# Hybrid encoder trunk, the scan: one predicated copy joins a level's inverse and its transpose; the opening merge is issued earlier

## The reference, cut to what matters

```python
L = jnp.where(strict, jnp.einsum('bhnik,bhnjk->bhnij', k_beta, k) * decay, 0.0)
sol = lax.linalg.triangular_solve(eye + L, rhs, left_side=True, lower=True)
...
def step(S, inp):                      # RWKV-7
    r_t, w_t, k_t, v_t, a_t, b_t = inp
    Sa = jnp.einsum('bhvk,bhk->bhv', S, a_t)
    S = S * w_t[:, :, None, :] + Sa[..., None] * b_t[:, :, None, :] + v_t[..., None] * k_t[:, :, None, :]
    return S, jnp.einsum('bhvk,bhk->bhv', S, r_t)
```

## Time and profile before

| | |
|---|---|
| runs | 4060.42, 4061.81, 4055.37 us; median 4060.42 |
| profiled execution | 4057.4 us, its span 4055.6 us |
| TensorE busy | 3793.7 us, 94% of the span |
| VectorE busy | 2142.2 us, 53% |
| ScalarE busy | 1305.0 us, 32% |
| GpSimd busy | 900.6 us, 22% |
| mean granted clock of TensorE | 0.965 of full speed |
| joins of the scan | 688.3 to 1410.3 us from the span's start |

### The profile page before, as it was taken

One profiled execution on the slowest core, in us unless ns is written; L12 is line 12 of the kernel. 1 busy time (PEld: TensorE's weight loads), 2 busy tenths in 40 slices (PEclk: granted clock), 3 DMA queues, 4 the chain that ended last, 5 costly groups with the idle time before them and its releaser, 6 DMA issues. The chain is left out here.

```text
span 4055.6 us, 74164 instructions
## 1 busy us (share of the span) xinstructions
PE 3793.7 (94%) x31136; PEld 3237.2 (80%) x31136; DVE 2142.2 (53%) x3226; ACT 1305.0 (32%) x2304; POOL 900.6 (22%) x472
## 2 busy tenths in 40 slices
PE   7999975999999988999999997899989899999998
PEld 6888854888888867888888886788868788888887
DVE  5644286767767785434333346566643343433335
ACT  3321274444344443111111114355533211111112
POOL 1231174111111033111111112134422211111113
PEclk8999976999999989999999997999999999999999
DMA  4322495222222152101101113000022110110112
GB/s 120 92 83 82 141 345 195 75 70 70 75 70 70 44 193 82 42 31 41 41 32 41 41 42 113 9 8 13 1 89 83 47 42 31 41 41 32 41 41 104
DMA packets 193526, 289.37 MB, mean 71 GB/s; under 512 B 31216, under 2 KB 134448, under 8 KB 193296
## 3 DMA queue, kind: packets, MB, share of 16 engines
q1 hardware_dynamic: 193296, 286.02, 21.1%
HBM read 207.99 MB, written 77.99 MB: 71 GB/s over the span
## 5 line engine op out<-in xcount | busy, mean ns | idle before, releaser
L847 DVE TENSOR_TENSOR top_acc<-top_acc,ffn_down 128x512 f32<-128x512 f32 x600 | 412.4, 687 | 358.4 <-PE ffn_down L112 357.7
L110 PE MATMUL ffn_up<-hT_ffn_high,ffn_w_high 128*128 128x512 f32 (+1 forms) x1536 | 544.0, 354 | 4.9 <-DVE hT_ffn_low L809 4.9
L112 PE MATMUL ffn_up<-hT_ffn_high,ffn_w_low 128*128 128x512 f32 (+1 forms) x1536 | 543.8, 354 | 0.0
L111 PE MATMUL ffn_up<-hT_ffn_low,ffn_w_high 128*128 128x512 f32 (+1 forms) x1536 | 543.5, 354 | 0.0
L110 PE MATMUL ffn_down<-ffn_w_high,ffn_f_high 128*128 128x512 f32 x1280 | 498.6, 390 | 0.0
L111 PE MATMUL ffn_down<-ffn_w_low,ffn_f_high 128*128 128x512 f32 x1280 | 498.3, 389 | 0.0
L112 PE MATMUL ffn_down<-ffn_w_high,ffn_f_low 128*128 128x512 f32 x1280 | 497.9, 389 | 0.0
L836 DVE TENSOR_TENSOR ffn_square<-ffn_relu 128x512 f32<-128x512 f32 (+1 forms) x192 | 146.6, 764 | 640.8 <-ACT ffn_relu L762 640.8
L110 PEld LDWEIGHTS ffn_up<-hT_ffn_high,ffn_w_high 128*128 128x128 f32 x1536 | 290.6, 189 | 46.3 <-issue 5.3
L111 PEld LDWEIGHTS ffn_up<-hT_ffn_low,ffn_w_high 128*128 128x128 f32 x1536 | 290.6, 189 | 40.9
L112 PEld LDWEIGHTS ffn_up<-hT_ffn_high,ffn_w_low 128*128 128x128 f32 x1536 | 290.5, 189 | 40.0
(11 more groups left out here) (477 smaller groups left out, 7948.7 us busy)
## 6 DMA issues: line engine op xcount, KB each, us to landing
up_w_raw<-in_w_ff SPq DMA_DIRECT2D x64, 1024.0 KB, 5.1
s_tm_both<-prepare_tb SPq DMA_DIRECT2D x20, 512.0 KB, 6.7
s_fm_dir<-prepare_fd SPq DMA_DIRECT2D x20, 512.0 KB, 6.9
scan_tb<-s_tm_both SPq DMA_DIRECT2D x20, 512.0 KB, 3.7
scan_fb<-s_fm_both SPq DMA_DIRECT2D x20, 512.0 KB, 4.8
scan_fd<-s_fm_dir SPq DMA_DIRECT2D x20, 512.0 KB, 5.9
up_w_raw<-s_x SPq DMA_DIRECT2D x20, 512.0 KB, 4.8
top_acc<-in_w_in_even SPq DMA_DIRECT2D x18, 512.0 KB, 5.5
```

The costliest lines, as they stand in the source:

```text
L110: pe.matmul(out, stationary[0], moving[0], start=start, stop=False)
L111: pe.matmul(out, stationary[0], moving[1], start=False, stop=False)
L112: return pe.matmul(out, stationary[1], moving[0], start=False, stop=stop)
L847: dve.tensor_tensor(a, a, out_of(u), ALU.add).then_inc(added, 1)
```

## The change

The two halves of X and of XT become one tensor of a quad, `XX`, in the order X half 0, XT half 0, X half 1, XT half 1. In this order the mixed pieces of X and of XT, and also the fixed ones, can be walked by one address pattern. Both products of a level go into one bank, the XT product behind the X product, and one `copy_predicated` of 128x512 joins both. Units alternate between banks 2 and 3, and so do the levels of quad 0. Four semaphores become two (`joined`, `g_joined`), and one wait for the bank two units back takes the place of two. The mask is kept once and repeated by the address pattern. In the opening `g_first` stands ahead of GpSimd's wait for `cleared`; of the seven tiles that VectorE cleared, ScalarE takes four, after its `decay_exp`.

```diff
-    Xp = [E.sb(f"X{q}", [P, 2, GR, HALF]) for q in range(Q)]
-    XTp = [E.sb(f"XT{q}", [P, 2, GR, HALF]) for q in range(Q)]
+    XX = [E.sb(f"X{q}", [P, 2, 2, GR, HALF]) for q in range(Q)]
+    Xp, XTp = [x[:, :, 0, :, :] for x in XX], [x[:, :, 1, :, :] for x in XX]
+    STRIDE = 2 * BLOCK
...
-    CLEARED = 27
-    DVE_TILES = 7
+    CLEARED = 28
+    DVE_TILES, ACT_TILES = 3, 7
...
+    def joint_halves(q, m):
+
+        n, rows = 1 << m, XX[q][:, :, :, :, :]
+        return bass.AP(rows.tensor, rows.offset + STRIDE, [rows.ap[0], [HALF, 2 * GR], [2 * n, HALF // (2 * n)], [n - STRIDE, 2], [1, n]])
+
+    def joint_mask(m):
+
+        n, rows = 1 << m, both_levels[:, m, :].bitcast(I32)
+        return bass.AP(rows.tensor, rows.offset, [rows.ap[0], [0, 2 * GR], [2 * n, HALF // (2 * n)], [n, 2], [1, n]])
+
+    def g_bank(m):
+
+        return 3 - m % 2
...
+    def joint_blocks(bank, m):
+
+        return ps[:, bank, 0:2 * BLOCK].rearrange("p (h a b n) -> p h a b n", h=2 * GR, b=2, n=1 << m)
...
                 if m < LAST:
-                    level(2, inner_blocks[0], gYc).then_inc(s["gz_product"], 1)
-                    level(3, gYc, inner_blocks[0]).then_inc(s["gzt_product"], 1)
+                    level(g_bank(m), 0, inner_blocks[0], gYc)
+                    level(g_bank(m), BLOCK, gYc, inner_blocks[0]).then_inc(s["gzt_product"], 1)
...
-                    pe.wait_ge(s["x_joined"], X_UNITS * i + u - RQ + 1)
+                    pe.wait_ge(s["joined"], UNITS * i + u - RQ + 1)
...
+                if u >= RQ:
+                    pe.wait_ge(s["joined"], UNITS * i + u - RQ + 1)
                 if m < LAST:
-                    if u > 0:
-                        pe.wait_ge(s["x_joined"], X_UNITS * i + u)
-                    level(2, inner_blocks[1 + u % 2], Y[u % 2]).then_inc(s["z_product"], 1)
-                if u > 0:
-                    pe.wait_ge(s["xt_joined"], UNITS * i + u)
-                if m < LAST:
-                    level(3, Y[u % 2], inner_blocks[1 + u % 2]).then_inc(s["zt_product"], 1)
+                    level(2 + u % 2, 0, inner_blocks[1 + u % 2], Y[u % 2])
+                    level(2 + u % 2, BLOCK, Y[u % 2], inner_blocks[1 + u % 2]).then_inc(s["zt_product"], 1)
...
-            act.activation(out[:, DVE_TILES:TILES, :].rearrange("p t (a n) -> p (t a) n", n=P), bcm(ident[:, :], (TILES - DVE_TILES) * D // P),
-                           ACT.Copy, scale=0.0).then_inc(s["cleared"], 1)
+            def clear_out(tiles):
+                act.activation(out[:, tiles, :].rearrange("p t (a n) -> p (t a) n", n=P), bcm(ident[:, :], (tiles.stop - tiles.start) * D // P),
+                               ACT.Copy, scale=0.0).then_inc(s["cleared"], 1)
+
+            clear_out(slice(ACT_TILES, TILES))
...
             for d in range(2):
                 decay_exp(0, 0, d)
+            clear_out(slice(DVE_TILES, ACT_TILES))
...
+            g_first(0, 0)
             pool.wait_ge(s["cleared"], CLEARED)
-            g_first(0, 0)
...
-            def join(x, bank, m):
-                return dve.copy_predicated(x, in_halves(both_levels[:, m, :, :], m).bitcast(I32), in_halves(out_blocks(bank), m))
+            def join(q, bank, m):
+                return dve.copy_predicated(joint_halves(q, m), joint_mask(m), joint_blocks(bank, m))
...
                 m, q = unit(u)
-                if m < LAST:
-                    dve.wait_ge(s["z_product"], X_UNITS * i + u + 1)
-                    join(x_halves(q, m), 2, m).then_inc(s["x_joined"], 1)
                 dve.wait_ge(s["zt_product"], UNITS * i + u + 1)
...
-                join(xt_halves(q, m), 3, m).then_inc(s["xt_joined"], 1)
+                join(q, 2 + u % 2, m).then_inc(s["joined"], 1)
```

More of the change, by code:

```diff
@@ L1470, in in_halves, with mixed_halves, out_block @@
         return ap.rearrange("p h (a b n) -> p (h a) b n", b=2, n=1 << m)
[L1472 removed]
+    def mixed_halves(pair, m, h=None, part=slice(0, P)):
         n, rows = 1 << m, pair[part, :, :, :]
         at, blocks = (0, BLOCK // (2 * n)) if h is None else (h * HALF, HALF // (2 * n))
[L1476 to L1477 removed]
+        return bass.AP(rows.tensor, rows.offset + STRIDE + at, [rows.ap[0], [2 * n, blocks], [n - STRIDE, 2], [1, n]])
     def x_halves(q, m, h=None, part=slice(0, P)):
[L1481 removed]
+        return mixed_halves(Xp[q], m, h, part)
     def xt_halves(q, m, h=None, part=slice(0, P)):
[L1485 removed]
+        return mixed_halves(XTp[q], m, h, part)
+    def joint_halves(q, m):
[6 more added lines that the diff above has]
+        return 3 - m % 2
     def both_columns(ap):
         return ap.rearrange("p h (a n) -> p (h a) n", n=HALF)
[L1491 to L1493 removed]
+    def out_block(bank, h, part, at=0):
+        return ps[part, bank, at + h * HALF:at + (h + 1) * HALF]
+    def joint_blocks(bank, m):
+        return ps[:, bank, 0:2 * BLOCK].rearrange("p (h a b n) -> p h a b n", h=2 * GR, b=2, n=1 << m)
     def out_blocks(bank, part=slice(0, P)):
@@ L1503, in last_xt @@
     def last_xt(q, h):
-        return XTp[q][UPPER, slot[0], h, :], XTp[q][LOWER, slot[1], h, :]
+        return XTp[q][UPPER, 1 - slot[0], h, :], XTp[q][LOWER, 1 - slot[1], h, :]
     def fixed_columns(pair, first, part=slice(0, P)):
         rows = pair[part, :, :, :]
-        step = BLOCK if first == 0 else -BLOCK
-        return bass.AP(rows.tensor, rows.offset + first * BLOCK, [rows.ap[0], [HALF, GR], [2, HALF // 2], [step + 1, 2]])
+        step = STRIDE if first == 0 else -STRIDE
+        return bass.AP(rows.tensor, rows.offset + first * STRIDE, [rows.ap[0], [HALF, GR], [2, HALF // 2], [step + 1, 2]])
     def ident_columns():
@@ L1597, in level_y, with level @@
                 return last
-            def level(bank, stationary, moving):
+            def level(bank, at, stationary, moving):
                 for h in range(GR):
                     for part in (LOWER, UPPER):
-                        last = pe.matmul(out_block(bank, h, part), stationary[part, h, :], moving[part, h, :], start=True, stop=True)
+                        last = pe.matmul(out_block(bank, h, part, at), stationary[part, h, :], moving[part, h, :], start=True, stop=True)
                 return last
@@ L1610, in last_y, with last_zt @@
                 return last
-            def last_zt(q, y):
+            def last_zt(q, y, bank):
                 for h in range(GR):
                     xt_fwd, xt_bwd = last_xt(q, h)
-                    pe.matmul(out_block(3, h, LOWER), y[UPPER, h, :], xt_fwd, start=True, stop=True)
-                    last = pe.matmul(out_block(3, h, UPPER), y[LOWER, h, :], xt_bwd, start=True, stop=True)
+                    pe.matmul(out_block(bank, h, LOWER), y[UPPER, h, :], xt_fwd, start=True, stop=True)
+                    last = pe.matmul(out_block(bank, h, UPPER), y[LOWER, h, :], xt_bwd, start=True, stop=True)
                 return last
@@ L3622, in constants @@
     row, column = s % mid, np.arange(mid)[None, :]
-    c["c_both_levels"] = np.stack([np.tile(row >> m == (column >> m) ^ 1, (1, 4)) for m in range(LEVELS - 1)]) * 1.0
+    c["c_both_levels"] = np.stack([row >> m == (column >> m) ^ 1 for m in range(LEVELS - 1)]) * 1.0
     keep = np.ones((2, P, TILES))
```

64 lines of the change are left out of this document (30 added, 34 removed).

## The result

The changed kernel takes **4077.17 us** (median of 5 runs, 4076.54 to 4081.13), against 4060.42 before: a ratio of 1.0044 with a 95% interval of 1.0033 to 1.0055. It is slower by 16.8 us, where 12.4 were forecast. The profiled execution took 4077.05 us with a span of 4075.3, 19.7 more than the span before.

The account below looks back on a forecast made before the run. It took the scan to be bound by TensorE's queue with short holes. 7.6 + 9.2 + 1 + 3.6 - 8.0 - 1 = +12.4 us gave 4072.8 against the median, slower at 0.57; the range takes in 4056 to 4084.

Parts of the forecast that it names:

- Price of the joint copy: VectorE's 128x512 join: result after 0.72 us, next start after 0.62; at the first level 1.2 and 1.05.
- Steps (1) to (3): Tail of a turn, g group's levels 3 to 5: later joins delay VectorE's masked copies 0.84 us, 7.6 over nine crossings.
- Steps (4) and (5): Units 0 and 1: Y of units 2 and 3 start 1.65 and 1.76 us later; ten times 0.92, 9.2 us.
- Step (6): Later units: nothing added or recovered; the last product's 0.59 us hole goes, worth 0 because the queue waits for GpSimd's merge.
- The last turn, +1: End of the scan: nothing fills the gaps of units 7 to 9 and one chain wait of 0.75 shows; +1 us.
- The opening's moved merge: Opening: GpSimd's merge starts 7.5 us sooner and its three instructions save 0.9 more; -8.0 us taken.
- The opening's chain, +3.6: Opening's levels: joint copies delay Y of level 2 by 1.3 us, later levels by 1.0, 0.75 and 0.54; +3.6 us.
- the clock, -1: Opening: TensorE's shorter idle stretch can bring the full clock sooner, taking back 1 of some 3 us.
- The rival of an opening that pays for the joins: No change, chance 0.28: two-element pieces cost nothing in the joint copy, so +2.7 us in all, 4063.1.
- That of a faster VectorE: Chance 0.15: VectorE sets the pace for part of a turn and joint copies pace below 0.62 us; 4038 us.

Follow-up runs that it names:

- two_copies: The changed kernel with its layout and opening, but X and XT of every level again in two banks with a copy each; 4051.52 us.
- group_split: The changed kernel with two copies in two banks for the g group's levels alone, the units keeping the joint copy; 4064.97 us.
- late_y: The kernel with two copies a level and the changed layout and opening, but Y's wait moved to the second (XT) copy; 4063.81 us.
- joint_only: The changed kernel with the opening of the kernel before; 4088.44 us.
- busy_opening: The changed kernel with 16 unread matmuls added in the opening, 11 ahead of the first product and 5 ahead of Y; 4072.79 us.
- opening_only: The kernel before with the change's opening alone, two copies a level in two banks staying; 4052.22 us.
- narrow_split: The changed kernel with two copies in two banks for the units' first level alone; 4070.66 us.
- fill_ahead: The changed kernel with 11 unread matmuls added ahead of the opening's first product alone; 4077.53 us.
- fill_between: The changed kernel with 5 unread matmuls added before Y of the opening's levels alone; 4073.29 us.
- busy_best: The kernel before with the change's opening alone, plus 16 unread matmuls in that opening; 4050.24 us, and 4050.66 when run again.

## Why the prediction came out as it did

The direction, the range and the mechanism of a turn were right; 12.4 us were forecast and 16.8 measured. By its own steps:

- **Price of the joint copy** (0.72 result and 0.62 pace; 1.2 and 1.05 at the first level): 0.73 and 0.63, 1.28 and 1.06 to 1.09. Right. The Trainium skill's "Vector Engine (DVE) Microarchitecture Reference" (5.2) would have runs of two adjacent words, if they start on an 8-byte boundary, at the full rate; the joint copy's rows speak against it. The Trainium skill's "VectorE: DVE Perf Modes" (TRN2 errata) has a fixed cost for each instruction with a source in SBUF (here the mask), not for every instruction as the prediction put it. In the pace of these rows one instruction fewer saves 0.05 us (two of 0.34 against 0.63), and with all 150 back two_copies is faster, since VectorE is not the bound.
- **Steps (1) to (3), +0.84 in the tail:** VectorE's masked copies start 29.39 behind KD instead of 28.42, +0.97, and group_split takes just that away. The join of level 4 started 0.46 late and not 0.28, so Y of level 4 was 0.77 late instead of 0.58. Shown besides, by late_y, is that the wide copy does this and not TensorE's wait.
- **Steps (4) and (5), +1.65 and +1.76:** Y of unit 2 is at 42.75 behind KD against about 40.92, +1.83, and Y of unit 3 at 46.51 against 44.54, +1.97. Of this 1.00 arises at the units (0.92 forecast). Nothing is recovered behind it, as said in (6).
- **Step (6), the last product's hole worth 0:** shown by two_copies, where the hole is gone and the turn is the same.
- **The last turn, +1 beside the turn's own loss:** too small. The last three Y wait 0.83, 0.83 and 0.82, where before one Y waited 0.51 and the last product 0.71, and 0.7 more passes in a hole without a releaser behind them: 4.2 in all instead of 2.8.
- **The opening's moved merge, -8.0:** the merge came 7.4 us sooner against the scan's start. -7.6 in the changed kernel, -8.5 and -7.4 in those with two copies. Right, although of the 0.9 that I had the three instructions save only 0.1 came: L2130 took 2.09 us beside VectorE's work instead of 1.28.
- **The opening's chain, +3.6, and the clock, -1: this is the step that failed.** joint_only is 7.4 longer up to KD 2, of which 1.0 is the units': the chain costs 6.4 and not 3.6, and the early start gives no clock back. I priced each delayed join by itself, with the clock as it was before, and even credited the clock. The chain with joint copies leaves TensorE holes of 0.8 to 1.4 us ahead of each Y that waits for one, and its clock came back 20 to 22 us behind the first product instead of nine. Most of the missing 2.8 us lies there. From the second join to the fourth the changed kernel took 9.36 us at the low clock and busy_opening 6.45 at the full one, 2.9 less, and before the change the clock was full from 692.7 on, as its second join ended (0.91 from 692 to 696). This is an estimate from one profile of each. That the holes are what kept the clock low fits the profiles but wasn't shown apart. The span grew by 7.3 more than forecast: 4.3 in this stretch, 2.7 in the eight turns (1.8 by the steps above, the rest in single longer turns), 1.4 in the last one, and -1.1 ahead of the scan.

The rival of an opening that pays for the joins fell with the price of the first level. That of a faster VectorE fell with the page's busy times: 13.7 us less work on it, and no turn shorter.

A version better than both is in the table: the opening alone, 4052.2 us, 0.9980 of before (0.9971 to 0.9989).

## What to carry over

A copy that joins two results in one instruction can start only when the later one is there, and it holds its engine longer at a time. Where its engine is the bound that may be a gain, which no run here shows; where TensorE waits for the result, as here, two short copies let the first consumer go and split the hold, although they cost more work. And a chain of small products with holes in it should be priced at the low clock too: here the same levels took 9.36 us at one level of the clock and 6.45 at the other.

## What the runs showed of the hardware

- TensorE's clock in the opening's chain, by one profile of each run. With Y behind the X copy alone it was full again 9 to 12 us behind the first product (before, opening_only, two_copies, group_split). With Y behind the second copy or a joint one it took 19 to 22 us (changed, joint_only, narrow_split, late_y, fill_ahead, fill_between). In seven profiles the clock was full at the first product: it stayed so in busy_opening and fell within 3.3 us in the six others (opening_only, group_split, fill_ahead, fill_between, busy_best twice). In busy_best it came back 12 and 16 us behind the first product.
- A predicated copy of 128x512 takes 0.73 us, and 1.28 with pieces of two elements taken in turn from two places of a tensor, whether as one copy or as two: 0.72 and 0.76 for two of 128x256.
- The same GpSimd addition (L2112, L2130) took 1.27 us in a turn, where VectorE ran predicated copies out of PSUM beside it, and 2.09 in the changed opening beside VectorE's additions of two tensors in SBUF. The two additions ahead of it took 1.27 and 1.28 there, mostly beside VectorE's clearing. VectorE paid as well: L2225 took 1.75 there and 0.69 in a turn.
